# A fused two-block kernel: expert layer 1 fed with raw transposed rows, its first gathers released pair by pair

## The reference

```python
h = h + (gate_a * y_a + gate_b * y_b) @ w_o            # mixer output, residual
x = rmsnorm(h, g_ffn)                                  # x = h * rsqrt(mean(h*h) + eps) * g_ffn
q = (x @ w_q).reshape(tokens, 8, 2, 128)               # 8 heads, 2 halves
s = einsum('thcd,hcnd->thcn', q, sub_keys)             # 128 scores for each half
top_s, top_i = top_k(s, 16)                            # then top 16 of the 16*16 sums
e = i1 * 128 + i2                                      # 16 experts for each head and token
act = gelu(einsum('td,ted->te', x, expert_u[e]))
y = einsum('te,ted->td', gate * act, expert_v[e])
h = h + y
```

## Time and profile before

| | |
|---|---|
| median of 3 runs | 2527.14 us (2520.34 to 2527.57) |
| the profiled execution | 2523.63 us, of which span 2521.8 us |
| PE busy | 2240.3 us (89%) |
| DVE busy | 1659.2 us (66%) |
| ACT busy | 912.2 us (36%) |
| POOL busy | 876.7 us (35%) |
| DMA | 945.41 MB, mean 375 GB/s |
| gathers | 805.36 MB in 110592 packets |

### The profile page before, as it was taken

How to read it: one execution, slowest core, us unless ns; L and a number is a source line. 1 busy time by engine, 2 the same in 40 slices (tenths; PEclk the granted TensorE clock), 3 DMA queues, 4 the chain that set the end, 5 groups by cost and what they waited for, 6 DMA issues and landing times.

```text
span 2521.8 us, 29577 instructions
## 1 busy us (share of the span) xinstructions
PE 2240.3 (89%) x9630; PEld 1259.0 (50%) x9630; DVE 1659.2 (66%) x3971; ACT 912.2 (36%) x2668; POOL 876.7 (35%) x796
## 2 busy tenths in 40 slices
PE   9989989989898989998989888889899999977776
PEld 7877745544454435554535454435545535522222
DVE  3864466666675677566776666667567767776664
ACT  2232233332343433343443234533345533423232
POOL 0022043334343334333343343334333444343342
PEclk9999999999999989999999999999999999999999
DMA  5421589999999999999999999999999999999996
GB/s 195 133 68 36 195 344 421 421 421 421 421 418 420 413 385 421 421 420 421 419 395 420 421 421 420 422 411 407 421 416 401 407 419 421 416 416 421 421 418 287
DMA packets 152442, 945.41 MB, mean 375 GB/s; under 512 B 16954, under 2 KB 19146, under 8 KB 53860
## 3 DMA queue, kind: packets, MB, share of 16 engines
q0 software_dynamic: 110592, 805.36, 77.2%
q1 hardware_dynamic: 41700, 138.20, 14.2%
HBM read 942.44 MB, written 1.05 MB: 374 GB/s over the span
## 4 chain that ended last, share of the span: by engine, by line
DMA 42%; PE 39%; DVE 9%; ACT 5%; issue 3%; POOL 1%; DVEq 0%; SPq 0%; ACTq 0%; POOLq 0%
DMA arena<-in_uv,idx 42%; PE bank L1882 22%; PE bank L354 6%; DVE arena L1910 5%; PE bank L1539 1%; ACT arena L1948 1%; PE bank L1527 1%; PE bank L848 1%; PE bank L827 1%; PE bank L585 1%; DVE arena L1198 1%; ACT arena L1936 1%; POOL arena L1967 1%; PE bank L814 1%; ACT arena L1942 1%
## 5 line engine op out<-in xcount | busy, mean ns | idle before, releaser
L1882 PE MATMUL bank<-arena 128*128 128x512 f32 x3072 | 1444.2, 615 | 252.6 <-ACT arena L1948 249.5
L1967 POOL DMA_INDIRECT arena<-in_uv,idx x768 | 849.0, 1105 | 1423.5 <-PE bank L1882 1293.3
L1882 PEld LDWEIGHTS bank<-arena 128*128 128x128 f32 x3072 | 572.4, 195 | 972.0 <-issue 601.7
L1910 DVE CUSTOM_DVE_ANT_0 arena<-arena,h 128x1024 f32<-128x1024 f32 x512 | 627.4, 1225 | 413.3 <-DMA arena<-in_uv,idx 410.6
L1936 ACT ACTIVATE arena<-arena 128x2 f32<-128x2 f32 x384 | 78.2, 204 | 1229.8 <-DVE arena L1910 1229.6
L1910 DVE CUSTOM_DVE_ANT_0 arena<-arena 128x1024 f32<-128x1024 f32 x256 | 313.8, 1226 | 218.5 <-DMA arena<-in_uv,idx 216.9
L354 PEld LDWEIGHTS bank<-xT,weights 128*128 128x128 f32 x2000 | 273.8, 192 | 55.8 <-issue 38.8
L354 PE MATMUL bank<-xT,weights 128*128 128x128 f32 (+2 forms) x2000 | 292.7, 302 | 0.0
L1948 ACT ACTIVATE arena<-const,arena 128x128 f32<-128x128 f32 x768 | 260.4, 386 | 0.0
L1942 ACT ACTIVATE arena<-arena 128x1 f32<-128x1 f32 x768 | 184.8, 288 | 12.6
L1936 ACT ACT_TABLE_LOAD x73 | 93.7, 1283 | 1.3
(11 more groups left out here) (331 smaller groups left out, 1768.6 us busy)
## 6 DMA issues: line engine op xcount, KB each, us to landing
weights<-in_w_q SPq DMA_DIRECT2D x50, 512.0 KB, 8.2
weights<-in_w_in SPq DMA_DIRECT2D x38, 512.0 KB, 3.4
weights<-in_a_fm SPq DMA_DIRECT2D x28, 512.0 KB, 10.0
arena<-in_uv,idx POOLq DMA_INDIRECT x768, 14.1
weights<-in_a_out SPq DMA_DIRECT2D x16, 512.0 KB, 7.8
weights<-in_b_fm SPq DMA_DIRECT2D x16, 512.0 KB, 8.0
weights<-in_b_out SPq DMA_DIRECT2D x16, 512.0 KB, 10.3
arena<-in_w_q SPq DMA_DIRECT2D x14, 512.0 KB, 13.5
```

What stands on the lines that cost most here:

```text
L1882: ins = nc.tensor.matmul(acc[:, :], diag[:, e % DIAGS, :], ring[:, e % RING, at:at + 512], start=first, stop=last)
L1910: V.tensor_tensor_reduce(out=u, in0=u, in1=x, scale=1.0, scalar=0.0, op0=ALU.mult, op1=ALU.add, accum_out=dots[:, unit % 2, kx:kx + 1]).th ...
L1967: nc.gpsimd.indirect_dma_start(out=ring[:, s, :], out_offset=None, in_=io[f"uv{unit // PH // NT}"], in_offset=bass.IndirectOffsetOnAxis(ap ...
```

## The change

Four things are altered. In tile order:

1. The transposes of expert layer 1 take `h` itself, not the normed row. The row's norm weight `g_ffn` is a per-partition factor after the transpose, so DVE multiplies it in while it copies to `xT` (`raw_in`, new, in place of ACT's copy). The row's root is a per-token factor and is applied by ACT as the scale of the score copy (`score_out`). The normed `xn` is still made for the dot products.
2. `w_o` moves to ring slots 3 to 6 and `mix` to slot 7. PE raises `w_o_pair_used` after every second kc block of tile 1's `mixed_out`; gathers 3, 4 and 5 wait for one pair each and gather 6 for the last.
3. The order around the start of the stream changes on PE, ACT and DVE: `rwkv_out(1, 0)` goes behind `early_head(0, 0)`, `early_head(1, 0)` ahead of `mixed_out(1)`, `early_head(2, 0)` behind stream step 0 on PE and behind step 1 on ACT, `last_residual_in` behind dot product 3, tile 1's norm to steps 2 to 5, and `mix_in(1, ...)` to two places inside unit 0's chain.
4. The pieces of heads 3 to 7 (`first_slot`) run one step later. SP loads w_o block 5 ahead of block 4.

```diff
@@ w_o and mix
-        mix = A.view(3 * 2 * D, KC, TOK)
-        w_o = A.view(4 * 2 * D, KC, D)
+        mix = A.view(7 * 2 * D, KC, TOK)
+        w_o = A.view(3 * 2 * D, KC, D)
@@ one_tensor
             rwkv_transposed(pe, 1)
-            rwkv_out(pe, 1, 0)
@@ mixed_out
+            if i and kc % 2 and kc < KC - 1:
+                ins.then_inc(sem("w_o_pair_used"), 1)
@@ one_vector
+            raw_in(v, 0)
             variance(v, 0, 0)
             first_apply(v, 0)
@@ raw_in, new
+        def raw_in(v, i):
+            at = COLS["g_ffn"][0]
+            for half in range(2):
+                v.wait_ge(*banks.full(("xT", 0, i, half)))
+                out = banks.bank(("xT", 0, i, half))
+                ins = nc.vector.tensor_tensor(xT[:, 4 * half:4 * half + 4, cols_of(i)],
+                                              out[:, :].rearrange("p (a b) -> p a b", a=4),
+                                              bc(cols[:, at + 4 * half:at + 4 * half + 4], (1, 4), (0, P)), ALU.mult)
+                ins.then_inc(banks.emptied_sem(("xT", 0, i, half)), 1)
@@ first_slot
-            return PH * group - 23 + step
+            return PH * group - 22 + step
@@ score_out
-            nc.scalar.activation(scores[:, at:at + (hi - lo) * NKEYS], out[:, 0:(hi - lo) * P], ACT.Copy).then_inc(
-                banks.emptied_sem(job), 1)
+            scale = 1.0
+            if job[1] == 0:
+                act.wait_ge(sem(f"norm_var_{i}"), 2)
+                scale = small[:, 2 + i:3 + i]
+            nc.scalar.activation(scores[:, at:at + (hi - lo) * NKEYS], out[:, 0:(hi - lo) * P], ACT.Copy,
+                                 scale=scale).then_inc(banks.emptied_sem(job), 1)
@@ first_tensor
-            fm_tensor(pe, 0, 0, xn)
+            fm_tensor(pe, 0, 0, h)
             fm_wait(pe, 0, 0)
             early_head(0, 0)
+            rwkv_out(pe, 1, 0)
             rwkv_out(pe, 1, 1)
+            early_head(1, 0)
             for kc in range(KC):
                 mixed_out(pe, 1, kc, (acc_lo, acc_hi), None)
-            early_head(1, 0)
+            yield 0
             early_head(2, 0)
             yield 1
-            fm_tensor(pe, 0, 1, xn)
+            fm_tensor(pe, 0, 1, h)
+            yield 2
             fm_wait(pe, 0, 1)
@@ first_scalar
-            fm_scalar(act, 0, 0)
             early_head(0, 0)
+            early_head(1, 0)
             softmax_exp(act, 0)
-            early_head(1, 0)
+            yield 1
+            early_head(2, 0)
+            yield 2
             norm_squares(act, 0, 1)
-            early_head(2, 0)
-            yield 0
+            yield 4
             norm_root(act, 0, 1)
-            yield 1
-            fm_scalar(act, 0, 1)
@@ stream_vector
-            mix_in(v, 1, 0)
             for n_op in range(TOPK_OPS):
                 next(ops)
-                if n_op == 11:
+                if n_op == 8:
+                    mix_in(v, 1, 0)
+                if n_op == 18:
                     mix_in(v, 1, 1)
-            last_residual_in(v)
...
+                    if e == 2 * GROUP - 1:
+                        last_residual_in(v)
@@ stream_gpsimd
-                    if e == 3:
+                    if 3 <= e < 6:
+                        pool.wait_ge(sem("w_o_pair_used"), e - 2)
+                    if e == 6:
                         pool.wait_ge(sem("w_o_last"), 2)
@@ beside_vector
-            yield 0
+            yield 3
+            raw_in(v, 1)
+            yield 4
             variance(v, 0, 1)
+            yield 5
             first_apply(v, 1)
```

More of the change, by code:

```diff
@@ L79 @@
                   ("conv_b", 4), ("conv_ln_g", 4), ("conv_ln_b", 4), ("conv_w", CT * TAPS),
-                  ("b_gate", 3), ("head_g", 6)):
+                  ("b_gate", 3), ("head_g", 6), ("g_ffn", 8)):
     COLS[_name] = (_n, _w)
@@ L1469, in normed @@
         def normed(engine, m, i):
-            if m == 0:
-                engine.wait_ge(sem(f"normed_{i}"), 1)
+            if m == 0 and i == 0:
+                for half in range(2):
+                    engine.wait_ge(*banks.emptied(("w_o", 0, half)))
+            elif m == 0:
+                engine.wait_ge(sem("w_o_last_added"), 2)
             else:
@@ L1505, in fm_scalar @@
                 out = banks.bank(("xT", m, i, half))
-                to = xw[:, 4 * half:4 * half + 4, :] if m else xT[:, 4 * half:4 * half + 4, cols_of(i)]
-                ins = nc.scalar.activation(to,
+                ins = nc.scalar.activation(xw[:, 4 * half:4 * half + 4, :],
                                            out[:, :].rearrange("p (a b) -> p a b", a=4), ACT.Copy)
                 ins.then_inc(banks.emptied_sem(("xT", m, i, half)), 1)
+        def raw_in(v, i):
+            at = COLS["g_ffn"][0]
+            for half in range(2):
+                v.wait_ge(*banks.full(("xT", 0, i, half)))
[4 more added lines that the diff above has]
+                ins.then_inc(banks.emptied_sem(("xT", 0, i, half)), 1)
         def plain(act, job, to, n=P, scale=1.0):
@@ L2811, in _ @@
                 sp.wait_ge(*banks.full(("O", 1, par)))
-            for kc in range(KC):
+            for kc in (0, 1, 2, 3, 5, 4, 6, 7):
+                if kc == 4:
+                    for par in range(2):
+                        sp.wait_ge(*banks.full(("SO", 1, par)))
                 sp.dma_start(w_o[:, kc, :], io["w_o"][kc]).then_inc(sem(f"w_o_in_{kc}"), 16)
@@ L2871, in lay_out @@
                                 i["conv_w"][0].reshape(TAPS, CT, P).transpose(2, 0, 1).reshape(P, -1),
-                                column(i["a_b_gate_2"][0]), column(i["a_head_g_2"][0].reshape(-1))], 1)
+                                column(i["a_b_gate_2"][0]), column(i["a_head_g_2"][0].reshape(-1)), column(i["g_ffn"][0])], 1)
     a["w_conv_out"] = half_fm_blocks(i["w_conv_out"][0])
```

## The result

The changed kernel takes 2534.71 us (median of 7 runs, 2529.74 to 2538.17) where the kernel before, run beside it, takes 2527.03 us (7 runs, 2520.34 to 2530.53). The ratio is 1.0034, with a 95% interval of 1.0021 to 1.0047: it is **slower by 0.34%**, and outside the predicted range. The profiled execution took 2534.02 us, span 2532.2 us.

A forecast was written before the change was run, and what follows sets the result against it. DMA, full once the gathers run, was taken as the bound. Gather 0 2.2 us earlier and 2.8 us less lost between gathers 7 and 18 made -5.0: 2527.1 - 5.0 = 2522.1 us, range 2515.5 to 2529.5.

The forecast's parts named there:

- What costs nothing: Side effects priced at no time: `w_o` in other bytes, eight more columns of constants, two `w_q` blocks loaded later.
- the sum: Whole kernel: start -2.2 us, loss between gathers 7 and 18 4.4 where it was 7.2, together -5.0 us.
- the end of the stream and the other windows move as a whole: Everything behind the joint only shifts in time, with no gain or loss of its own.
- the rivals: Gain beyond 7.6 us, 0.22; only 2.2 us or nothing gained, 0.25; slower by over 0.3%, 0.08.
- (c): Later score pieces of heads 3 to 7 come too late in every unit: up to +7.5 us; slower, any cause, 0.08.
- Step 1: Indices of unit 0: transposes wait for the addition alone, indices ready at 314.3, 2.2 us earlier, gather 0 at 314.6.
- Step 2: Gathers 1 to 7: gather 3 due at 318.5, gather 7 issued 1.2 us later than before, at no cost.
- Releasing by pairs is what makes this so: Release by `mixed_out` pairs issues gathers 3 to 7 early enough to cost nothing; wins nothing beyond the 2.2 us.
- Step 3: Wait for `v_used(0)`: PE waits 5.6 us, clock falls, gather 8 at 336.5; 1.0 us lost, 3.6 before.
- Step 4: Head 2 inside the stream delays gather 10 to 344.8: 3.4 us lost; DVE waits some 8 us for exponentials.
- 0 to 2: Loss in us at gathers 12 and 14 together, behind gather 10; taken as 0 in the sum.
- A rule against this change: ACT table switches cost 1380 ns more drain each, making the gain 2.2 us and not 5.0; chance 0.02.

The follow-up runs named there:

- run 1: Kernel before with 8 unused floats behind `cols`, giving it the changed kernel's addresses: 2541.57 us, 1.0053 of the kernel before.
- run 3: Changed kernel with 56 unused floats behind `cols`, weight slots at 0 and ring at 192 past 256: 2521.16 us, 0.9980 of the kernel before.
- run 7: Kernel of run 3 with the pair release undone, gathers 3 to 7 waiting for the last w_o block: 2525.82 us, 1.0009 of the kernel before.
- Run 8: Kernel of run 3 with head 2 ahead of the stream on PE and behind step 0 on ACT: 2518.97 us, 0.9975 of the kernel before.
- run 4: Kernel before with 16 unused floats behind `cols`, weight slots at 64 and ring at 0 past 256: 2504.42 us, 0.9910 of the kernel before.
- run 6: Kernel before with 16 unused floats ahead of the ring alone, ring on a multiple of 256: 2497.31 us, 0.9912 of the kernel before.
- run 17: Changed kernel with 56 unused floats directly ahead of `weights`, slots at 0 and ring at 192 past 256: 2524.30 us, 0.9991 of the kernel before.
- run 13: Changed kernel with 56 unused floats ahead of the ring alone, slots at 32 and ring at 192 past 256: 2530.13 us, 1.0014 of the kernel before.
- run 18: Kernel before with weight slots moved 32 bytes on and the ring kept at 192 past 256: 2537.31 us, 1.0043 of the kernel before.
- run 5: Kernel before with 8 unused floats ahead of the ring alone, ring at 224 past 256: 2533.43 us, 1.0040 of the kernel before.
- run 14: Kernel before with 72 unused floats ahead of the ring, again 224 past 256 but 256 bytes further on: 1.0024 of the kernel before.

## Why the prediction was wrong, by its own steps

**The step that failed** stands in "What costs nothing": "eight more columns of constants". I priced their transfer and not their place. They moved the weight slots off a multiple of 256 bytes and the ring from 192 to 224 past one. With the schedule held fixed that costs 1.0053 (run 1) or, in the changed kernel, 1.0034/0.9980 = 1.0054: 0.54% or 13.6 us of 2527. The forecast of 2522.1 us was met by the changed kernel with its old addresses, 2521.16 us (run 3). That it was met within 1 us is partly luck, as the interval of run 3's ratio alone is 5 us wide and one term of the sum was too small (below).

The sentence "the end of the stream and the other windows move as a whole" failed with it: they hold 16.0 us more, in this pair of executions. None of the rivals had this mechanism. (c), the one on the slower side, named the score pieces. It isn't what happened: DVE waits 7.9 us in 1920 for score copies, and it waits the same 7.9 us in run 3, which is faster than the kernel before though its pieces come a step later as well.

**What was right.** The rest, by terms:
- Step 1, -2.2: measured -4.33 (316.82 to 312.49) with 2.1 of it from the mixer ahead, so -2.2. Run 3's trace has it too: 21.54 us from the last residual addition to gather 0, where the kernel before has 23.77. `raw_in` was 0.2 cheaper than taken.
- Step 2: gather 3 goes at 316.38 (318.5 less 2.1). "Releasing by pairs is what makes this so": undone, it costs 4.5 us (run 7).
- Step 3: PE waits 5.61 us (5.6), the clock falls, gather 8 goes at 333.99 (334.4).
- Step 4: gather 10 goes at 342.82 (342.7), though the first pair took 6.16 us and not 5.6. DVE's wait for the exponentials is 9.96 us (8 taken). Run 8 takes the stall away and wins 4.3 us, beside the 1.0 + 3.4 of the sum.
- The sum: from gather 0's issue to gather 18's landing 59.9 became 58.6, a gain of 1.3 where I had 7.2 - 4.4 = 2.8. The missing 1.5 lie almost all behind gather 10, where I had "0 to 2" and took 0: gather 10 lands at 342.82 + 5.8 = 348.6 (348.3 by the sum), and from there to gather 18 it takes 22.5 us, where eight at 2.5 and the weight block's 1.2 make 21.2. With step 1 it is 3.5 us in this trace; three pairs of medians say about 5, with an interval that holds 3.5.
- "A rule against this change", the drain at each switch of tables, doesn't show after the change either: the load for the exponentials takes 1.28 us from 343.58, and the exponential starts at 344.88.

**The form of the loss.** In 380 to 684 us, full queues here move 425 to 427 GB/s into a ring on a multiple of 256 bytes and 418 to 422 elsewhere. The Trainium skill (DMA: Bandwidth & Descriptors, How a descriptor splits into AXI transactions) says that a descriptor which does not start on a multiple of 256 bytes pays for a first transaction from the boundary below its start. My estimate from its beats of 32 bytes, if a row of 8 KB is one descriptor, is 0.4% more at 32 bytes past (257 beats for 256), 2.3% at 192 and 2.7% at 224. The trace agrees that the multiple is the cheap place, and not on the form: 32 costs as much as 192, and the step to either is 0.9% of the time. The page words it for what is read; here only the written side was moved.

**What stays open**: why 224 is worse than 192, why the slots cost at 32 and not at 64 (run 4's 0.9910 beside run 6's 0.9912), and whether the 0.1% between runs 17 and 3, whose intervals overlap, belongs to `h` and `xT`. Two more comparisons bear on the last, in which the changed kernel has `h` and `xT` 32 bytes on and the kernel before has not, at equal slots and ring: run 17 gives 0.9991 and run 13 against run 18 gives 1.0014/1.0043 = 0.9971. They lie on either side of run 3's 0.9980, so no steady loss from `h` and `xT` shows. Nor was the place of the slots parted from that of `rows` and `idx`, which moved with them in runs 17 and 18. That it is the writes of the queues, and not another effect of the same addresses, rests on where the rate falls, not on a transfer measured by itself.

## What to carry to other kernels

Where a stream of transfers is the bound, print the start address of every array that it writes, before and after each edit, and keep ring and load slots on multiples of 256 bytes with a pad of their own, so that no edit to a small table ahead of them can move them. Test a change of schedule at equal addresses; otherwise one measures the sum of two things, here -0.2% and +0.54%. And when a time moves without a new wait, compare the rate of the full queues slice by slice: a loss that is even over all slices points away from the schedule.

## What was not expected of the hardware

- The rate of full queues depends on the ring's start: 425 to 427 GB/s on a multiple of 256 bytes, 420 to 422 at 192 past, 418 to 421 at 224 past (slices 1 to 8, the kernel before and runs 5, 6 and 14). One line of padding, without any change of order, makes this tuned kernel 0.9% faster (run 6).
- Weight slots of 4 KB rows that start 32 bytes past a multiple of 256 cost 0.43% of the whole (run 18, with `rows` and `idx` moved as well), though hardware queue 1, which writes them, carries 83 of 631 MB in the stretch compared. In the changed kernel the same move costs 0.23% (run 13 against run 17).
